# Expert layers of a two-layer model on one core: 416 tokens accumulated densely in eight PSUM banks, 104 tokens fetching their own value rows

## The reference, cut to what matters

```
q = (x @ w_q).reshape(t, 8, 2, 128)                 # 8 heads, two halves
s = einsum('thpd,phkd->thpk', q, sub_keys)          # 128 scores per half
sv, si = top_k(s, 16)
cand = sv[:, :, 0, :, None] + sv[:, :, 1, None, :]  # 16 x 16 pairs
top_s, top_pos = top_k(cand, 16);  g = softmax(top_s)
idx = si_first * 128 + si_second                    # of 16,384 experts
act = gelu(u_tab[idx] . x)                          # one hidden number per pick
y = sum over the 8 x 16 picks of g * act * v_tab[idx]
```

## Time and profile before

| | |
|---|---|
| device time, median of 3 runs | 4712.9 us (4711.35 to 4715.23) |
| span of the profiled execution | 4713.5 us |
| PE busy | 4391.2 us, 93% of the span, 33,800 matmul records |
| DVE busy | 2862.9 us, 61% |
| ACT busy | 1151.9 us, 24% |
| POOL busy | 5.3 us, 11 instructions |
| transfers | 625.63 MB, mean 133 GB/s |

### The profile page before, as it was taken

The page is one execution under the profiler, slowest core; times in us unless marked ns, Lnnn a source line. Parts: engine busy times, 40 slices in busy tenths (PEclk is TensorE's granted clock), DMA queues, the critical chain, the costliest instruction groups (busy, mean ns, idle before and its releaser), DMA issues. The chain is left out here.

```text
span 4713.5 us, 91695 instructions
## 1 busy us (share of the span) xinstructions
PE 4391.2 (93%) x33800; PEld 4208.7 (89%) x33800; DVE 2862.9 (61%) x6816; ACT 1151.9 (24%) x1581; POOL 5.3 (0%) x11
## 2 busy tenths in 40 slices
PE   8677997889999999999999896889999999999998
PEld 8656676889999999999998846889999999999997
DVE  3641104877766734677776474977776634677775
ACT  2100003123333321211111344133333322111111
POOL 0000000000000000000000000000000000000000
PEclk9876768999999999999999998999999999999999
DMA  3012421135544563455552201135544463555552
GB/s 109 14 65 99 169 90 68 61 93 176 169 140 149 167 215 108 160 186 180 185 180 100 74 16 67 49 105 177 172 157 146 149 218 103 172 187 188 180 185 81
DMA packets 256621, 625.63 MB, mean 133 GB/s; under 512 B 22401, under 2 KB 104450, under 8 KB 255874
## 3 DMA queue, kind: packets, MB, share of 16 engines
q1 hardware_dynamic: 247298, 603.21, 38.8%
q10 hardware_dynamic: 9216, 20.98, 1.2%
HBM read 492.05 MB, written 131.93 MB: 132 GB/s over the span
## 5 line engine op out<-in xcount | busy, mean ns | idle before, releaser
L1169 PE MATMUL ps<-peer_xh,peer_ul 128*128 128x260 f32 x4096 | 1171.2, 286 | 49.4 <-DVE peer_ul L1380 32.5
L1170 PE MATMUL ps<-peer_xl,peer_uh 128*128 128x260 f32 x4096 | 1159.5, 283 | 0.0
L1171 PE MATMUL ps<-peer_xh,peer_uh 128*128 128x260 f32 x4096 | 1158.4, 283 | 0.0
L1169 PEld LDWEIGHTS ps<-peer_xh,peer_ul 128*128 128x128 f32 x4096 | 775.2, 189 | 50.2 <-DVE peer_ul L1380 32.9
L1170 PEld LDWEIGHTS ps<-peer_xl,peer_uh 128*128 128x128 f32 x4096 | 775.5, 189 | 0.0
L1171 PEld LDWEIGHTS ps<-peer_xh,peer_uh 128*128 128x128 f32 x4096 | 775.0, 189 | 0.0
L1735 PE MATMUL ps<-experts_gh,experts_vh 128*128 128x260 f32 x2304 | 650.7, 282 | 0.0
L1734 PE MATMUL ps<-experts_gl,experts_vh 128*128 128x260 f32 x2304 | 649.7, 282 | 0.0
L1733 PE MATMUL ps<-experts_gh,experts_vl 128*128 128x260 f32 x2304 | 649.2, 282 | 0.0
L1832 DVE TENSOR_TENSOR peer_out_r<-peer_out_r,ps 128x520 f32<-128x520 f32 x512 | 354.6, 693 | 432.5 <-PE ps L1735 432.5
L1380 DVE TENSOR_TENSOR peer_ul<-peer_u,peer_uh 128x1024 fp32r<-128x1024 f32 x220 | 269.2, 1224 | 453.6 <-ACT peer_uh L1516 450.1
(11 more groups left out here) (325 smaller groups left out, 6914.4 us busy)
## 6 DMA issues: line engine op xcount, KB each, us to landing
peer_u<-peer_u SPq DMA_DIRECT2D x256, 512.0 KB, 3.9
experts_v<-peer_v SPq DMA_DIRECT2D x256, 512.0 KB, 3.3
gates<-gates_g SPq DMA_DIRECT2D x80, 832.0 KB, 5.8
experts_g<-gates SPq DMA_DIRECT2D x64, 1040.0 KB, 7.2
hidden<-gates_hid SPq DMA_DIRECT2D x216, 260.0 KB, 4.1
experts_act<-hidden SPq DMA_DIRECT2D x216, 260.0 KB, 3.5
pa_ct<-cache ACTq DMA_DIRECT2D x64, 320.0 KB, 7.8
pa_ct<-cache SPq DMA_DIRECT2D x64, 320.0 KB, 8.2
```

The costliest lines, as they stand in the source:

```text
L1169: pe.matmul(o, self.ul[:, b, c], self.xh[:, c, t], start=(c == 0), stop=False)
L1170: pe.matmul(o, self.uh[:, b, c], self.xl[:, c, t], start=False, stop=False)
L1171: mm = pe.matmul(o, self.uh[:, b, c], self.xh[:, c, t], start=False, stop=(c == KC - 1))
```

## The change

It touches only the expert layers.

- Output: tokens 0 to 415 (`ND`, 4 tiles) are one product of 416 columns, accumulated in 8 PSUM banks (one per chunk of output values) over all 128 blocks. A block is 24 matmuls. The banks are read once, at the end. `r` goes away; the sum goes to `k.x`.
- Tokens 416 to 519 (the last tile) have no dense gates. Their picks become addresses. In the experts stage POOL issues 128 indirect transfers of hidden numbers (104 x 4 bytes, `fetch_cell`, in batches of 16) and 128 of value rows (104 x 4 KB, `fetch_row`, 4 buffers), and DVE adds each weighted row to an accumulator (`add_rows`, one SCALAR_TENSOR_TENSOR of 104 x 1024), 6 blocks behind the dense work. At the end PE turns the accumulator into columns.
- All 128 hidden blocks are computed in the gates stage; the experts stage has outputs alone.
- The gates stage selects for the last tile first, then for the 4 dense ones, 30 hidden blocks a tile (22 of them spread over the 26 banks). `uh` and `ul` are three deep. PE waits for a tile's selection after 6 hidden blocks of it. One TENSOR_TENSOR of 1,024 elements makes the one-hots of a bank, and ACT weighs them (`weigh`, four scaled copies of 128). All loops but PE's over the output blocks are written out.
- In the experts stage ACT makes `gh`, buffers of `v`, hidden and gated values are 4 deep.

The core of the diff:

```diff
 # gates stage, DVE
+                def one_hot(q):
+                    at = 4 * (q % banks)
+                    if q >= 2:
+                        v.wait_ge(g_ready, q - 1)
+                    v.tensor_tensor(one[:, q % 2], bc(cols[:, 0:2, at:at + 4], 3, NK), bc(bc(k.iota[:], 1, 4), 1, 2),
+                                    ALU.is_equal).then_inc(one_ready, 1)
...
+                for t in range(NDT):
+                    select(t + 1, t, first(t) + 3).then_inc(ijg_ready, 1)   # splits first+3 .. first+8 inside
                     v.wait_ge(turned, t + 1)
+                    chain(v.tensor_copy(cols[:], turn))
+                    one_hot(banks * t)
+                    split(first(t) + SELECT + 1)
+                    split(first(t) + SELECT + 2)
+                    step = first(t) + SELECT
+                    for n in range(banks):
+                        if n + 1 < banks:
+                            one_hot(banks * t + n + 1)
+                        for _ in range(share(n, banks, late)):      # late = 22
+                            split(step + 3)
+                            step += 1
 # gates stage, PE
+                for t in range(NDT):
+                    for n in range(SELECT - 2):
+                        hidden(first(t) + n)
                     pe.wait_ge(ijg_ready, t + 1)
...
+                    hidden(first(t) + SELECT - 2)
+                    hidden(first(t) + SELECT - 1)
+                    for n in range(banks):
+                        gates(banks * t + n)                        # waits for weighed_ready
+                        for _ in range(share(n, banks, late)):
+                            hidden(step)
 # gates stage, ACT
+                def high(s):
+                    if s >= 3:
+                        act.wait_ge(h_ready, s - 2)
+                    act.activation(uh[:, s % 3], u[:, s % 2], ACT.Copy).then_inc(u_high, 1)
+                def step(s):
+                    high(s + 3)
+                    act.wait_ge(h_ready, s + 1)
+                    act.activation(halves(hid[:, s % 2]), ..., ACT.Gelu).then_inc(gelu_ready, 1)
+                    weigh(banks * t)
+                    for n in range(banks):
+                        if n + 1 < banks:
+                            weigh(banks * t + n + 1)
+                        for _ in range(share(n, banks, late)):
+                            step(at)
+                            at += 1
+                        copy_gates(banks * t + n)
 # gates stage, SP, after the last hidden block
+                for c in range(STORES):
+                    store_gates(NDT - 1, c)
+                sp.wait_ge(g_stored, 16 * STORES * NDT)
 # experts stage
+            def _(pool):
+                for q in range(PICKS):
+                    if q % BATCH == 0:
+                        for n in range(q, q + BATCH):
+                            ga.fetch_cell(pool, ..., n)
+                    ga.fetch_row(pool, ..., q)      # from the 5th on waits for the buffer: used >= q - 3
+            def _(pe):
+                def output(n, b, first=False, last=False):
+                    for c in range(KC):
+                        o = k.ps[:, c, 0:ND]
+                        pe.matmul(o, wl[:, b, f], gh[:, b], start=first, stop=False)
+                        pe.matmul(o, wh[:, b, f], gl[:, b], start=False, stop=False)
+                        mm = pe.matmul(o, wh[:, b, f], gh[:, b], start=False, stop=last)
```

More of the change, by code:

```diff
@@ L1372, in peer_gates, with first @@
         banks = TT // 4
[L1373 to L1374 removed]
+        late = PER_TILE - SELECT
+        def first(t):
+            return SELECT + PER_TILE * t
         with s.block() as block:
@@ L1377, in _, with split, select @@
             def _(v):
[L1378 to L1401, removed]
+                chain = Chain(v, link)
+                def split(s):
+                    if s < NK:
+                        v.wait_ge(u_high, s + 1)
+                        v.tensor_tensor(ul[:, s % 3], u[:, s % 2], uh[:, s % 3].bitcast(F32), ALU.subtract
+                                        ).then_inc(u_split, 1)
+                def one_hot(q):
[4 more added lines that the diff above has]
+                                    ALU.is_equal).then_inc(one_ready, 1)
+                def select(t, tile, ahead):
+                    val = values[:, tile].rearrange("t (h p) r -> t h p r", p=2)
+                    rank = ranks[:, tile].rearrange("t (h p) r -> t h p r", p=2)
                     v.tensor_tensor(cand[:, :, 0:CANDA * 16].rearrange("t h (x y) -> t h x y", y=16),
@@ L1460, in _ @@
-                    chain(v.tensor_copy(cols[:], turn), base)
-                    assert chain.n == 15
-                    split(ahead + 6, 6)
-                    with v.Fori(0, rounds) as u:
-                        for b in range(0, 4, 2):
-                            one_hot(t, 4 * u, b)
-                            one_hot(t, 4 * u, b + 1)
-                            split(ahead + 2 * u + 7 + b // 2, 7 + b // 2)
-                    one_hot(t, 4 * rounds, 0)
-                    one_hot(t, 4 * rounds, 1)
@@ L1470, in _ @@
-                    split(ahead + PER_TILE - 1, PER_TILE - 1)
-                for b in range(EXTRA):
-                    split(PER_TILE * NT + 2 + b, b)
+                        ins = v.tensor_tensor(pick[:], bc(r[:].rearrange("t h r -> t (h r)"), 2, TOPK),
+                                              bc(iota16, 1, PICKS), ALU.is_equal)
+                        split(ahead + 4 + p)
+                        chain(ins)
+                        of_head = pick[:].rearrange("t (h r) x -> t h r x", h=PH)
@@ new lines, in _ @@
+                for n in range(3):
+                    split(n)
+                chain(select(0, NDT, 3))
+                v.tensor_copy(ga.gate[:], ijg[:, 2])
+                chain(v.tensor_scalar(ijg[:, 0], ijg[:, 0], float(NK), None, ALU.mult))
+                chain(v.tensor_tensor(ijg[:, 0], ijg[:, 0], ijg[:, 1], ALU.add))
+                v.tensor_scalar(ga.row[:], ijg[:, 0], float(layer * NK * NK), None, ALU.add)
+                v.wait_ge(token_ready, 1)
+                chain(v.tensor_scalar(ga.cell[:], ijg[:, 0], float(T), token[:], ALU.mult, ALU.add))
@@ new lines, in _ @@
+                for b in range(4):
+                    output(b, b, first=(b == 0))
+                with pe.Fori(1, NK // 4 - 1) as i:
+                    for b in range(4):
+                        output(4 * i + b, b)
+                for b in range(4):
+                    output(NK - 4 + b, b, last=(b == 3))
+                pe.wait_ge(acc_ready, 1)
+                for c in range(KC):
+                    if c % 4 == 0:
+                        pe.wait_ge(y_free, c // 4 + 1)
+                    mm = pe.transpose(k.ps[:, c // 4, c % 4 * TT:(c % 4 + 1) * TT], acc[:, 0, c * P:(c + 1) * P],
+                                      k.ident[0:TT, 0:TT])
@@ L1895, in conv_module @@
+        layer_norm(nc, k, f"ln{layer}1", k.x, f"ln_g{layer}1", f"ln_b{layer}1", k.x, ACT.Identity,
+                   slabs(k, a["w_pw1"]) if layer == 0 else ())
 def conv_module(nc, k, a, h, r):
```

636 lines of the change are left out of this document (262 added, 374 removed).

## The result

The changed kernel takes 5019.3 us, median of 3 runs (5013.6 to 5033.6). Beside it the kernel before took 4712.9. The ratio is 1.0654, 95% interval 1.0639 to 1.0669: slower by 6.5%, where 4628 us (faster by 1.8%) was forecast. The time also lies outside the range of 4530 to 4765.

The account below looks back on a forecast made before the run. The prediction took PE's stream to bound both expert stages. Savings of 181.8 and 23.5 us less added waits, low clock and ends gave -42.4 us a layer, -85 over two: 4628 us from 4713.5, range 4530 to 4765.

Parts of the forecast that it names:

- Transfers: ... 1.38 MB, 4.17 us at 330 GB/s. Just hidden: Experts stage: a block's loads and fetched rows, 1.38 MB, take 4.17 us, hidden under PE's 4.32 us.
- transfers set the pace: Rival, chance 0.10, experts stage: at 300 GB/s a block takes 4.59 us and the kernel 4697 us.
- POOL: Rival, chance 0.27: POOL's indirect transfers, assumed 1.2 us each, set the experts stage's pace; at 1.6 us, kernel 4683 us.
- The reasoning from the batch: Experts stage: 16 hidden fetches in a row between row fetches cost nothing up to 1.41 us per indirect transfer.
- No idle time in the experts stage: Experts stage: DVE, ACT and transfers all hide under PE's 4.32 us block, so PE never idles there.
- The pitch: Output matmuls of 416 columns start 180 ns apart: -181.8 us a layer (-143 to -196).
- the rival of 0.04: Rival, chance 0.04: 416-column matmuls cost in proportion, 191.4 ns, making the kernel 4698 us, so the change saves nothing.
- The selection wait: Gates stage: PE waits 10.2 us for each of 4 tiles' selections; with 2.6 of low clock each, +51.2 us a layer.
- The bank wait: Gates stage: PE waits 3.8 us at four banks a tile that have no hidden block, +60.8 us a layer.
- Between the stages: From gates to experts stage: unhidden gate store and reload raise 8.5 us to about 34, +25.5 us a layer.
- The clock after bank waits: Gates stage: low PE clock costs 1.7 us after each of 12 bank waits, +20.4 us a layer (0 to 20).
- The end: End of the experts stage: 8 PSUM reads and two for the turned rows follow the last matmul, +5 us a layer.

## Why the prediction was wrong

- **The step that failed** is "Transfers: ... 1.38 MB, 4.17 us at 330 GB/s. Just hidden". The bytes were right (173.4 MB in 128 blocks, 1.35 each), the rate wasn't: 241 GB/s in the stage, 273 with all engines busy, where 1.38 MB take 5.0 us and PE's block 4.56. The 330 of the earlier trace rows is the rate of a window with 8 large stores, and no run shows it for fetched rows. It was the rival "transfers set the pace", given 0.10 and priced at 4697 us by 300 GB/s, that came true, at a far higher price: 682 us against 583 without rows. These 98 us and the 37 of the batch are most of the layer's 187.9. The rival's own remark, that rows of one transfer don't divide evenly by 16, should have been priced. The Trainium skill (DMA: Bandwidth & Descriptors, Why a DMA increments its semaphore by 16 and not by 1) states that a transfer is cut over the largest number up to 16 that divides the slowest dimension of both its sides, 13 for 104 rows and 16 for 96 or 112; this agrees with 682 us for 104 rows against 599 and 625, and with the 13 small packets of a transfer from SP and the 13 packets under way there. The trace doesn't say which engine moved a packet, and the scattered rows show no 13, so that this is the cause is argued, not shown.
- **POOL** (0.27) was the wrong rival alone and a right one in part: the price of 1.2 us was low (1.3 at best, 1.56 in the mean). The reasoning from the batch shows where it bites, as 37 us in layer 0 on top of full transfers, and nothing where the transfers have room.
- **No idle time in the experts stage** also meant no low clock there but the 2.6 us at its start. It is 30.8 us. Not every idle time brings it: PE idles 3.3 us between 2210 and 2255 at a mean clock of 1.00, and 11.4 in the next 45 us, at 0.85.
- **The pitch** of 180 ns was taken between bounds of 175.5 and 191.4, by the row of float32 streams whose overhead shrinks. 190 was measured: the nearest row in kind, 260 columns of the same product, should have decided. +30.7 us a layer, the rival of 0.04. (Its bound of -143 should read -147: 734.8 less 3072 x 0.1914.)
- **The selection wait**: 10.2 forecast, 10.1 measured, 4 times. **The bank wait**: 3.8 forecast, 4.0 at the 12 places, 2.9 and about 0.7 at the four first ones. **Between the stages**: 34 forecast, 30.7. Counting the chain of engines row by row held.
- **The clock after bank waits** was sized by 1.7 us each, 20.4 in all, from a row after which it was low for 3.4 us. Behind one wait of 4.0 us it is low for such a stretch here too (1118.3 to 1121.8, 0.53); behind another of the same length PE works at 0.50 and then 0.58 for 6.3 us. The low clock behind the bank waits costs 44.1 us in all, 2.8 each over 16, where 12 were priced. That behind the selection waits costs 8.1, 2.0 each where 2.6 was counted.
- **The end**: +9.2 for +5.

A gates stage with its waits mended and a stage of 583 us would have made the change worth it; as made, 175 us a layer are taken from PE (583.7 for 734.8, and 23.5 of gates) and some 320 added in waits, low clock and ends.

## What to carry to other kernels

When a dense product is replaced by fetched rows, count the transfer engines' time in packets beside the loads already there, not bytes at the best rate seen, and try row counts that are a multiple of 16. When two streams of work are woven over three engines, put what the other stream waits for ahead of anything that waits itself, and let the asking engine ask last: that order alone was worth 6% here. Price the idle times of PE with the low clock that can follow them; here it added half of the idle time again in the gates stage (52.2 us to 103.0), and a quarter in the experts stage.

## What the runs showed of the hardware

- An indirect transfer of 104 addresses occupies POOL 0.97 to 3.03 us and 0.30 pass before the next. The mean is 1.26 us at 4 bytes an address; at 4 KB it is 1.45 into one pair of buffers and 1.05 into the other, 1.25 together.
- A 4 KB packet of the loads took 160 ns without the rows (0.54 share), 186 to 220 beside them; a packet of a fetched row 222 to 263.
- Indirect transfers of 104 rows gave a stage of 682 us, of 112 rows 625, of 96 rows 599; plain transfers of 104 rows 738 from SP and 618 from POOL. A transfer of 104 rows brought 13 small packets from SP, 24 as a plain one from POOL and 40 as an indirect one, one of 96 or 112 rows 16.
- The pitch of these matmuls: 112 ns at 208 columns, 119.6 at 260, 190 at 416.
- After about 4 us idle within a dense stream PE worked at the 1.2 GHz level for a while: 3.5 us at a mean of 0.53 in one place, 6.3 us at 0.50 and then 0.58 in another.
